# The last dense coefficient block kept in SBUF, and the expert stage's buffers moved, in a two-layer decoder trunk

## The chip, the cores and the metric

The kernel runs on one core of one Trainium2 chip. Its time is the device time of one launch in microseconds (us). Three runs of it are shown, and one further execution was recorded by the hardware profiler.

## What is computed

The reference is a decoder trunk of two layers on 512 tokens of width 1024, in f32. A layer is a mixer (sliding-window attention beside a convolution) and then PEER, a retrieval of single-neuron experts. The change touches only PEER and the code around it:

```python
def peer(h, w_query, sub_keys, u_tab, v_tab):
    q = (xt @ w_query).reshape(T, 8, 2, 128)
    s = einsum('thpd,hpnd->thpn', q, sub_keys)          # 128 keys per half
    ... top 16 of each half, top 16 of the pair sums -> ids (T, 8, 16), gates = softmax(top_s)
    a = gelu(einsum('chkd,cd->chk', u_tab[idc], xc))     # 16384 experts in all
    coef = gc * a
    return einsum('chk,chkd->cd', coef, v_tab[idc])
```

So each token uses 128 of 16384 experts (8 heads x 16), and expert (i, j) is row 128*i + j of the two tables.

## The kernel before, in words

**Two ways for PEER.** The first 128 tokens are done sparsely: GpSimd gathers the rows of their experts (`gather`, L484), VectorE takes the dot products (`dot`, L1290) and later the weighted sum (`weigh`, L1443). The other 384 tokens (`ND`) are done densely: all 128 tiles of the first table are multiplied with all dense tokens, and the coefficients of the experts that a token did not choose are zero.

**The U stage** has 128 tiles, U0 to U127. For each, SyncE loads 512 KB into one of four slots (`load`, L361, waits for the product four tiles earlier), ScalarE casts it to the high part `w_hi` (L756), VectorE or GpSimd makes the low part `w_lo` (L1406, L439), TensorE multiplies (24 matmuls of 384 columns, L526 to L528), ScalarE applies Gelu (L942) and stores the result to DRAM, `gelu_scratch` (L944). U0 to U31 run in a loop while VectorE works out the routes of the tokens. Then TensorE transposes the routes (L692), once for each of the three blocks of 128 dense tokens, and VectorE copies them out as `ijg` (L1416).

**The dense coefficients C** are built during U32 to U127, one block of 128 tokens in each 32 tiles. A block has 16 groups of 8 tokens. For a group VectorE writes one-hot matrices (L1428, L1429, L1431), TensorE multiplies them (L706), and ScalarE copies the result into `stage` (L967), 64 KB in each partition, `[i, j, token]`. TensorE and ScalarE do group g after tile `group_tile(g)`, whose offsets in a block are `k*27//16`: 0, 1, 3, 5, 6, 8, 10, 11, 13, 15, 16, 18, 20, 21, 23, 25. VectorE's order is written out by hand: before the one-hot matrices of a group it makes every `w_lo` up to the tile after the group's, and after them two or three of the dot products.

```python
while lows <= min(group_tile(g) + 1, NKEYS - 1):   # L1421
    u_low(lows); lows += 1
```

Two tiles after the last group of a block, SyncE starts to store `stage` to `c_scratch`, 2 MB behind each of four successive loads (L390). ScalarE may not write the first group of the next block until all four have landed (L963). TensorE runs these 96 tiles as a loop of three passes (`pe.Fori(0, NBD)`, L695), a pass being one block; SyncE loops likewise (L383).

**The V stage** (`experts`, L712) has 128 tiles too. For tile j SyncE fetches column j of C, 192 KB from `c_scratch`, and 192 KB of `gelu_scratch` into `cg` (`load_cg`, L392). VectorE multiplies the two into `coef` (`mix`, L1451), ScalarE casts `coef` to `cf_hi` (`coef_high`, L977), VectorE makes `cf_lo` (`mixed_low`, L1458) and the tile's `w_lo` (`weight_low`, L1464), and TensorE does 24 matmuls of 384 columns (L716 to L718) that add up in all eight PSUM banks. `cg`, `coef`, `cf_hi`, `cf_lo` and `y_sp` (the sparse sum) lie where `stage` was, at `base`, so the four stores of the last block have to land first: ScalarE waits for them at L972 and then sets `cg_free` by 4 (L973), which lets SyncE ask for the first columns. VectorE waits for a column, clears `y_sp` (L1480) and begins. During the first 96 V tiles the adaLN rows of the next norm are loaded too (`load_rows`, L366) and reduced by VectorE (`modulate`, L1029).

Of the kernel before, what the change touches and what calls it, by code (L numbers as in the profile page):

```python
# [44 lines left out]
C_TILES = 32  # L45
# [40 lines left out]
def group_tile(g):  # L86

    return U_ROUTE + C_TILES * (g // (P // GROUP)) + group_offset(g % (P // GROUP))


def group_offset(k):
    return k * 27 // 16
# [35 lines left out]
def build_trunk(nc, stream, u_rows, ada, params_d, keys_d, con_d, x_d, c_d, pos_d, c_scr, g_scr, out_d):  # L128
    with ExitStack() as ctx:
# [19 lines left out]
        xT = keep("xT", [P, C, T])  # L149
        h_hi = keep("h_hi", [P, C, T], F32R)  # L150
# [17 lines left out]
        sinT = keep("sinT", [P, T])  # L168
        rstd = keep("rstd", [P, T])
# [64 lines left out]
        cg = at("cg", base, [P, 4, 2, ND])  # L234
        coef = at("coef", base + 16 * KB, [P, 2, ND])
        cf_hi = at("cf_hi", base + 20 * KB, [P, 4, ND], F32R)
        cf_lo = at("cf_lo", base + 36 * KB, [P, 4, ND], F32R)
        y_sp = at("y_sp", base + 32 * KB, [P, D])
# [109 lines left out]
        def _(sp):  # L348
# [11 lines left out]
            with sp.Fori(0, DEPTH) as l:  # L360
# [5 lines left out]
                def load_rows(s, g, used):  # L366
                    n = sp.snap(g)
                    sp.wait_ge(mod_step, used)
                    sp.dma_start(rows[s][:], ada[n]).then_inc(ada_in[s], 16)
# [13 lines left out]
                with sp.Fori(0, NBD) as tb:  # L383
                    for k in range(C_TILES):
                        load(k % 4, l * NT + I_U + U_ROUTE + 4 + C_TILES * tb + k)
                        part = k - group_offset(P // GROUP - 1) - 2
                        if 0 <= part < 4:
                            to = sp.snap(tb + 0)
                            sp.wait_ge(c_ev, l * 2 * GROUPS + 2 * (P // GROUP) * tb + 2 * (P // GROUP) + 4)
                            sp.dma_start(c_scr[bass.ds(to, 1), :, 32 * part:32 * part + 32].rearrange("b i j t -> i (b j) t"),  # L390
                                         stage[:, 32 * part:32 * part + 32]).then_inc(c_st, 16)
                def load_cg(s, j, k):  # L392
                    jj = sp.snap(j)
                    sp.wait_ge(cg_free, k)
                    sp.dma_start(cg[:, s, 0].rearrange("i (b t) -> i b t", b=NBD),
                                 c_scr[:, :, bass.ds(jj, 1)].rearrange("b i o t -> i (b o) t")).then_inc(cg_in[s], 16)
                    sp.dma_start(cg[:, s, 1], g_scr[jj]).then_inc(cg_in[s], 16)


                for s in range(4):  # L400
                    load_cg(s, s, l * (NKEYS + 4) + s + 1)
                for n in range(ADA_2, ADA_2 + 3):
                    load_rows(n % 4, l * ADA_ALL + n, l * ADA_ALL + n - 2)

                def w_loads(r, rows_left=4):
                    for k in range(16):
                        load_cg(k % 4, 16 * r + k + 4, l * (NKEYS + 4) + 16 * r + k + 5)
                        if k % 4 == 0 and k // 4 < rows_left:
                            n = ADA_2 + k // 4 + 3
                            load_rows(n % 4, l * ADA_ALL + n + 4 * r, l * ADA_ALL + n - 2 + 4 * r)  # L410
                        load(k % 4, l * NT + I_W + 16 * r + k + 4)

                with sp.Fori(0, 3 * C // 4 - 1) as r:
                    w_loads(r)
                w_loads(3 * C // 4 - 1, 1)
# [91 lines left out]
        def _(pe):  # L507
            pe.wait_ge(const_in, 64)
            with pe.Fori(0, DEPTH) as l:
# [177 lines left out]

                u_tiles(0, U_ROUTE)
                for tt in range(1, NB):
                    pe.wait_ge(rt_ready, l * NBD + tt)  # L690
                    for k in range(3):
                        mm = nc.tensor.transpose(ps[:, 2 + tt, k * P:(k + 1) * P], routed[:, tt, k], ident)  # L692
                    mm.then_inc(rt_tr, 1)

                with pe.Fori(0, NBD) as tb:  # L695
                    g = 0
                    for k in range(C_TILES):
                        product(k % 4, l * NT + I_U + U_ROUTE + C_TILES * tb + k,
                                l * (NE // 2) + (I_U + U_ROUTE) // 2 + C_TILES // 2 * tb + k // 2 + 1, h_hi, h_lo, t0=P)
                        if g < P // GROUP and group_offset(g) == k:  # L700
                            pe.wait_ge(lr_done, l * GROUPS + P // GROUP * tb + g + 1)
                            for q in range(2):
                                pe.wait_ge(c_ev, l * 2 * GROUPS + 2 * (P // GROUP) * tb + 2 * g + q + 1)
                                for t in range(4):
                                    slot = GROUP * (g % 2) + 4 * q + t
                                    mm = nc.tensor.matmul(ps[:, 2 + (2 * g + q) % 4, t * P:(t + 1) * P],  # L706
                                                          oneL[:, slot], oneR[:, slot], start=True, stop=True)
                                mm.then_inc(c_mm, 1)
                            g += 1

# [869 lines left out]
```

## Time and profile before

| | |
|---|---|
| three runs, us | 4071.08, 4075.35 (median), 4086.86 |
| the profiled execution, us | 4082.31 |
| its span on the core, us | 4080.5 |
| granted TensorE clock, mean | 0.947 |
| TensorE matmul busy | 3671.6 us, 90% |
| TensorE weight load busy | 3286.8 us, 81% |
| VectorE busy | 3169.2 us, 78% |
| ScalarE busy | 1543.8 us, 38% |
| GpSimd busy | 1867.9 us, 46% |
| DMA | 895.76 MB, 220 GB/s mean |

The profile is of one execution, on the one core, and the other tables are taken from its trace. Engines are PE (TensorE matmul), PEld (its weight load), DVE (VectorE), ACT (ScalarE), POOL (GpSimd) and SP (SyncE); a name with q is that engine's instruction queue, where DMA issues show. A wait is put down to the instruction that ended it; "issue" stands where the profile shows nothing that the engine waited for. Starts are us from the start of the span. A matmul's recorded duration is longer than its share of the time, since matmuls overlap: their starts tell the pace. The same holds for VectorE instructions in a row, which start 0.08 us before the one ahead is shown to end.

### The profile page before, as it was taken

Reading aid. Unit: us, or ns where it says so; the run is one execution under the profiler, and the core shown is the slowest. Engines: PE = TensorE matmul, PEld = TensorE weight load, DVE = VectorE, ACT = ScalarE, POOL = GpSimd, SP = SyncE. Lnnn points to the kernel's source line nnn. Section 1 sums busy time; section 2 is a strip of 40 time slices with the busy share of each in tenths; the row PEclk is TensorE's granted clock in tenths of the full one; section 3 lists DMA queues with packets and bytes.
Section 4 is the critical chain, followed back from the end, with each engine's and each line's share of the span. In section 5 each row is a group of like instructions: output and inputs, shape, how many; then the busy total and the mean of one; then the engine's idle time right before and its main releaser. Section 6 shows DMA issues by size and latency. Waiting matters only on the chain.

```text
span 4080.5 us, 61011 instructions
## 1 busy us (share of the span) xinstructions
PE 3671.6 (90%) x19042; PEld 3286.8 (81%) x19042; DVE 3169.2 (78%) x5223; ACT 1543.8 (38%) x2201; POOL 1867.9 (46%) x1324
## 2 busy tenths in 40 slices
PE   4888888998999969999978888889989999699998
PEld 2655666898999969999955556668989999699998
DVE  6888952799877958888768889328997979588887
ACT  3344233344444433333343332433444544233332
POOL 3211455365544645555432115544744646455553
PEclk9887999999999989999998779999999999899999
DMA  5410122256898899999933102223669898999997
GB/s 197 145 37 31 67 68 87 81 182 195 272 319 312 280 346 377 370 377 357 339 120 114 37 27 76 69 86 98 183 208 313 288 325 285 359 377 374 373 351 280
DMA packets 368728, 895.76 MB, mean 220 GB/s; under 512 B 33665, under 2 KB 197505, under 8 KB 364929
## 3 DMA queue, kind: packets, MB, share of 16 engines
q1 hardware_dynamic: 257632, 572.25, 40.8%
q0 software_dynamic: 73728, 268.47, 19.0%
q10 hardware_dynamic: 37152, 52.45, 3.5%
q8 instruction: 102, 1.67, 0.2%
q14 instruction: 114, 0.93, 0.1%
HBM read 790.27 MB, written 102.76 MB: 219 GB/s over the span
## 4 chain that ended last, share of the span: by engine, by line
PE 39%; issue 31%; DVE 14%; POOL 9%; DMA 6%; ACT 1%; SPq 0%; POOLq 0%; DVEq 0%; ACTq 0%
PE ps L716 8%; PE ps L718 8%; PE ps L717 8%; POOL w_lo L439 7%; PE ps L528 4%; PE ps L527 4%; PE ps L526 4%; DMA raw<-stream 3%; PE ps L706 3%; DVE i L1308 2%; DVE eq L1375 1%; DMA c_scratch<-stage 1%; DVE eq L1368 1%; DVE v L1304 1%; DMA cg<-gelu_scratch 1%
## 5 line engine op out<-in xcount | busy, mean ns | idle before, releaser
L526 PE MATMUL ps<-h_hi,w_hi 128*128 128x384 f32 (+1 forms) x3008 | 1115.2, 371 | 96.1 <-POOL h_lo L446 41.9
L439 POOL TENSOR_TENSOR w_lo<-raw,w_hi 128x1024 fp32r<-128x1024 f32 x232 | 638.3, 2760 | 1010.6 <-ACT w_hi L756 998.8
L527 PE MATMUL ps<-h_lo,w_hi 128*128 128x384 f32 (+1 forms) x3008 | 1078.4, 358 | 0.0
L528 PE MATMUL ps<-h_hi,w_lo 128*128 128x384 f32 (+1 forms) x3008 | 1076.8, 358 | 0.0
L756 ACT CAST w_hi<-raw 128x1024 fp32r<-128x1024 f32 x680 | 714.0, 1054 | 930.1 <-DMA raw<-stream 883.2
L716 PE MATMUL ps<-cf_hi,w_hi 128*128 128x384 f32 x2048 | 688.4, 336 | 67.8 <-DVE cf_lo L1461 65.9
L502 POOL TENSOR_TENSOR spare<-spare 128x1 f32<-128x1 f32 x504 | 282.9, 561 | 962.4 <-DVE y_sp L1448 487.4
L526 PEld LDWEIGHTS ps<-h_hi,w_hi 128*128 128x128 f32 x3008 | 578.9, 192 | 178.4 <-issue 52.1
L718 PE MATMUL ps<-cf_hi,w_lo 128*128 128x384 f32 x2048 | 685.9, 335 | 0.0
L717 PE MATMUL ps<-cf_lo,w_hi 128*128 128x384 f32 x2048 | 685.9, 335 | 0.0
L527 PEld LDWEIGHTS ps<-h_lo,w_hi 128*128 128x128 f32 x3008 | 580.1, 193 | 43.8 <-issue 8.0
L528 PEld LDWEIGHTS ps<-h_hi,w_lo 128*128 128x128 f32 x3008 | 577.7, 192 | 42.2
L487 POOL DMA_INDIRECT gbuf<-stream,ids_v x256 | 444.2, 1735 | 39.2 <-issue 2.6
L716 PEld LDWEIGHTS ps<-cf_hi,w_hi 128*128 128x128 f32 x2048 | 385.9, 188 | 73.9 <-DVE w_lo L1467 73.4
L487 POOL DMA_INDIRECT gbuf<-u_rows,ids_u x256 | 407.8, 1593 | 39.8 <-POOL spare L502 5.0
L717 PEld LDWEIGHTS ps<-cf_lo,w_hi 128*128 128x128 f32 x2048 | 385.9, 188 | 0.0
L718 PEld LDWEIGHTS ps<-cf_hi,w_lo 128*128 128x128 f32 x2048 | 385.7, 188 | 0.0
L1406 DVE TENSOR_TENSOR w_lo<-raw,w_hi 128x1024 fp32r<-128x1024 f32 x192 | 233.3, 1223 | 168.6 <-ACT w_hi L756 168.5
L1296 DVE CUSTOM_DVE_ANT_1 gbuf<-gbuf,h_tok 128x1024 f32<-128x1024 f32 x256 | 302.2, 1220 | 43.7 <-DMA gbuf<-u_rows,ids_u 43.7
L1448 DVE SCALAR_TENSOR_TENSOR y_sp<-gbuf,a_sp,y_sp 128x1024 f32<-128x1024 f32 x256 | 327.3, 1279 | 0.0
L1467 DVE TENSOR_TENSOR w_lo<-raw,w_hi 128x1024 fp32r<-128x1024 f32 x256 | 311.8, 1218 | 0.0
L942 ACT ACTIVATE g_out<-ps 128x384 f32<-128x384 f32 x256 | 125.8, 492 | 486.1 <-PE ps L528 474.8
(209 smaller groups left out, 4720.5 us busy)
## 6 DMA issues: line engine op xcount, KB each, us to landing
raw<-stream SPq DMA_DIRECT2D x680, 512.0 KB, 5.2
rows<-ada SPq DMA_DIRECT2D x112, 512.0 KB, 5.8
gelu_scratch<-g_out ACTq DMA_DIRECT2D x256, 192.0 KB
c_scratch<-stage SPq DMA_DIRECT2D x24, 2048.0 KB, 16.7
cg<-c_scratch SPq DMA_DIRECT2D x256, 192.0 KB, 5.4
cg<-gelu_scratch SPq DMA_DIRECT2D x256, 192.0 KB, 5.9
gbuf<-u_rows,ids_u POOLq DMA_INDIRECT x256, 6.6
gbuf<-stream,ids_v POOLq DMA_INDIRECT x256, 7.4
```

The costliest lines, as they stand in the source:

```text
L439: nc.gpsimd.tensor_tensor(w_lo[:, s], raw[:, s], w_hi[:, s].bitcast(F32), ALU.subtract).then_inc(lo_done, 1)
L487: nc.gpsimd.indirect_dma_start(out=gbuf[:, n % SLOTS], out_offset=None, in_=table, in_offset=bass.IndirectOffsetOnAxis(ap=ids[:, k:k + 1], ...
L526: nc.tensor.matmul(ps[:, b, 0:n], wh, hi[:, c, t0:T], start=c == 0, stop=False)
L527: nc.tensor.matmul(ps[:, b, 0:n], wh, lo[:, c, t0:T], start=False, stop=False)
L528: mm = nc.tensor.matmul(ps[:, b, 0:n], wl, hi[:, c, t0:T], start=False, stop=c == C - 1)
L716: nc.tensor.matmul(ps[:, c, P:T], w_hi[:, s, c], cf_hi[:, s], start=first, stop=False)
L717: nc.tensor.matmul(ps[:, c, P:T], w_hi[:, s, c], cf_lo[:, s], start=False, stop=False)
L718: mm = nc.tensor.matmul(ps[:, c, P:T], w_lo[:, s, c], cf_hi[:, s], start=False, stop=last)
L756: nc.scalar.copy(w_hi[:, s], raw[:, s]).then_inc(hi_done, 1)
L1296: nc.vector.tensor_tensor_reduce(out=row, in0=row, in1=h_tok[:, :, 0:P], scale=1.0, scalar=0.0, op0=ALU.mult, op1=ALU.add, accum_out=a_sp[ ...
L1448: nc.vector.scalar_tensor_tensor(out=y_sp[:], in0=gbuf[:, k % 4], scalar=a_sp[:, bass.ds(at_k, 1)], in1=y_sp[:], op0=ALU.mult, op1=ALU.add ...
L1467: nc.vector.tensor_tensor(w_lo[:, k % 4], raw[:, k % 4], w_hi[:, k % 4].bitcast(F32), ALU.subtract).then_inc(lo_done, 1)
```

## The change

1. The last of the three blocks of C is no longer stored. `c_scratch` has two blocks (`STORED`), the third stays in `stage`, and `mix` does two multiplications: 256 tokens from `cg`, 128 from the column of `stage`.
2. The V stage's buffers leave the place of `stage`: `cg` and `coef` to where the one-hot matrices were, `cf_hi` and `cf_lo` beside them and into `rstd` and `h_lo`, `y_sp` into `h_lo`, and the adaLN rows of the V stage (`w_rows`) into `h_hi`. The rows can be asked for only after the last U product, so `load_rows` goes behind `load` in the V stage, and `modulate` from the first to the last tile of four.
3. ScalarE sets `cg_free` after the last group, and SyncE asks for the first four columns during the last four U tiles. The waits of TensorE for banks 0 and 1 go to the last chunks of the first V tile. `coef_high(0, 0)` comes ahead of the Gelu of `a_sp` and ahead of the wait for the last stores of `gelu_scratch`; VectorE clears `y_sp` and finishes `a_sp` behind the first `mixed_low`.
4. The routes are transposed after U34 in place of after U31.
5. The groups of the blocks begin at tiles 36, 66 and 96 (before 32, 64 and 96), at offsets `k*23//16`: 0, 1, 2, 4, 5, 7, 8, 10, 11, 12, 14, 15, 17, 18, 20, 21.
6. The loops of TensorE and SyncE over the blocks are written out: no jump back at U64 and U96.

```diff
 def group_tile(g):
-    return U_ROUTE + C_TILES * (g // (P // GROUP)) + group_offset(g % (P // GROUP))
+    return C_FIRST[g // (P // GROUP)] + g % (P // GROUP) * 23 // 16
...
-        cg = at("cg", base, [P, 4, 2, ND])
-        coef = at("coef", base + 16 * KB, [P, 2, ND])
...
-        y_sp = at("y_sp", base + 32 * KB, [P, D])
+        cg = at("cg", base + 74 * KB, [P, 4, NS + ND])
+        coef = at("coef", base + 84 * KB, [P, 2, ND])
...
+        y_sp = at("y_sp", h_lo_base, [P, D])
+        w_rows = [at(f"w_rows{k}", h_hi_base + 4 * KB * k, [P, D]) for k in range(4)]
...
-                    sp.dma_start(cg[:, s, 0].rearrange("i (b t) -> i b t", b=NBD),
+                    sp.dma_start(cg[:, s, 0:NS].rearrange("i (b t) -> i b t", b=STORED),
                                  c_scr[:, :, bass.ds(jj, 1)].rearrange("b i o t -> i (b o) t")).then_inc(cg_in[s], 16)
...
-                for s in range(4):
-                    load_cg(s, s, l * (NKEYS + 4) + s + 1)
...
+                for u in range(U_ROUTE + 4, NKEYS + 4):
+                    load(u % 4, l * NT + I_U + u)
+                    for tb in range(STORED):
+                        part = u - 4 - group_tile((tb + 1) * (P // GROUP) - 1) - 2
+                        if 0 <= part < 4:
+                            sp.wait_ge(c_ev, l * 2 * GROUPS + 2 * (P // GROUP) * (tb + 1) + 4)
+                            sp.dma_start(c_scr[tb, :, 32 * part:32 * part + 32],
+                                         stage[:, 32 * part:32 * part + 32]).then_inc(c_st, 16)
+                    if u >= NKEYS:
+                        load_cg(u - NKEYS, u - NKEYS, l * (NKEYS + 4) + u - NKEYS + 1)
...
+                for u in range(U_ROUTE, NKEYS):
+                    u_tile(u)
+                    if u == U_ROUTE + 2:
+                        for tt in range(1, NB):
+                            pe.wait_ge(rt_ready, l * NBD + tt)
...
+                    while g < GROUPS and group_tile(g) == u:
+                        c_group(g)
+                        g += 1
+                W_ORDER = tuple(range(2, C)) + (0, 1)
...
+                    for c in W_ORDER:
+                        if first and c < 2:
+                            pe.wait_ge(bank_read[c], (l + 1) * (NE // 2) + 1)
...
-                act.wait_ge(c_st, (l + 1) * (NBD * 64) + 64)
-                nc.scalar.copy(st4[:, 4], st4[:, 3]).then_inc(cg_free, 4)
...
+                        if g == GROUPS:
+                            nc.scalar.copy(st4[:, 4], st4[:, 3]).then_inc(cg_free, 4)
...
+                coef_high(0, 0)
                 act.wait_ge(row_used, l * 2 * P + P + 4)
                 nc.scalar.activation(a_sp[:], a_sp[:], ACT.Gelu).then_inc(a_gelu, 1)
...
                 u_low(U_ROUTE + 1)
-                lows = U_ROUTE + 2
+                u_low(U_ROUTE + 2)
+                lows = U_ROUTE + 3
...
-                    nc.vector.tensor_tensor(coef[:, k % 2], cg[:, k % 4, 0], cg[:, k % 4, 1],
-                                            ALU.mult).then_inc(cg_free, 1)
+                    nc.vector.tensor_tensor(coef[:, k % 2, 0:NS], cg[:, k % 4, 0:NS], cg[:, k % 4, NS:2 * NS], ALU.mult)
+                    nc.vector.tensor_tensor(coef[:, k % 2, NS:], stage[:, bass.ds(j, 1)].rearrange("i o t -> i (o t)"),
+                                            cg[:, k % 4, 2 * NS:], ALU.mult).then_inc(cg_free, 1)
```

## Rows read from the trace of the kernel before

**Rows 1.** All waits of PE, whole span: us in total, times, longest
```profile
PE ps L716 <- DVE cf_lo L1461: 65.9, 2, 33.5
...
PE ps L706 <- DVE oneR L1431: 18.2, 22, 1.8
...
PE ps L526 <- issue: 11.8, 3, 4.7
```
**Rows 2.** The chain that ended last, in order of time: start us, us, what
```profile
987.39 1.78 PE ps L706 x16
...
1151.05 3.10 PE ps L706 x16
...
1476.84 28.67 DMA c_scratch<-stage
```
**Rows 3.** Waits from 1477 to 1514, then the same from 3491 to 3529
```profile
ACT st L973 <- DMA c_scratch<-stage: 13.8, 1, 13.8
...
PE ps L716 <- DVE cf_lo L1461: 32.4, 1, 32.4
```
**Rows 4.** Timelines of SP, DVE and PE around the first V tile
```profile
1505.81 0.40 SPq L395 DMA_DIRECT2D cg<-c_scratch  x1
...
1513.05 0.55 DVE L1461 TENSOR_TENSOR cf_lo<-coef,cf_hi 128x384 fp32r<-128x384 f32 x1
...
1513.73 0.68 PE L716 MATMUL ps<-cf_hi,w_hi 128*128 128x384 f32 x1 [33.49 <-DVE cf_lo L1461]
```
**Rows 5.** Timeline of ACT, U58 to U67: Gelus, casts and copies
```profile
1112.62 0.49 ACT L942 ACTIVATE g_out<-ps 128x384 f32<-128x384 f32 x1 [2.19 <-PE ps L528]
1113.14 0.34 ACTq L944 DMA_DIRECT2D gelu_scratch<-g_out  x1
1113.52 1.05 ACT L756 CAST w_hi<-raw 128x1024 fp32r<-128x1024 f32 x1 [0.41 <-ACT g_out L942]
1116.78 0.49 ACT L942 ACTIVATE g_out<-ps 128x384 f32<-128x384 f32 x1 [2.21 <-PE ps L528]
...
1137.12 1.05 ACT L756 CAST w_hi<-raw 128x1024 fp32r<-128x1024 f32 x1 [5.83 <-DMA raw<-stream]
...
1145.20 1.05 ACT L756 CAST w_hi<-raw 128x1024 fp32r<-128x1024 f32 x1 [6.64 <-DMA raw<-stream]
...
1152.96 1.05 ACT L756 CAST w_hi<-raw 128x1024 fp32r<-128x1024 f32 x1 [0.53 <-DMA raw<-stream]
```
**Rows 6.** DMA issues with sizes: KB, median us from issue to landing
```profile
cg<-gelu_scratch SPq DMA_DIRECT2D x256, 192.0 KB, 5.9
```
**Rows 7.** Timeline of DVE, one group of the first block
```profile
1020.28 1.22 DVE L1428 TENSOR_TENSOR oneR<-con,ijg 128x1024 f32<-128x1024 f32 x1
1021.41 1.22 DVE L1429 TENSOR_TENSOR oneL<-con,ijg 128x1024 f32<-128x1024 f32 x1
```
**Rows 8.** Timeline of SP: the loads and stores behind U61 and U62
```profile
1129.40 0.33 SPq L364 DMA_DIRECT2D raw<-stream  x1
1130.22 0.80 SPq L390 DMA_DIRECT2D c_scratch<-stage  x1
1133.56 9.87 SPq L364 DMA_DIRECT2D raw<-stream  x2
```
**Rows 9.** Timeline of PE from 1136 to 1152: the start of U64
```profile
1136.89 0.44 PE L526 MATMUL ps<-h_hi,w_hi 128*128 128x384 f32 x1 [3.51 <-issue]
```
**Rows 10.** Timeline of PE and DVE around the transposes of the routes
```profile
952.36 0.82 PE L692 MATMUL ps<-con,routed 128*128 128x128 f32 x6
962.82 0.90 PE L692 MATMUL ps<-con,routed 128*128 128x128 f32 x3 [9.64 <-DVE routed L1396]
963.95 0.69 PE L526 MATMUL ps<-h_hi,w_hi 128*128 128x384 f32 x1 [0.23 <-DVE w_lo L1406]
...
964.95 1.48 DVE L1416 COPY ijg<-ps 128x384 f32<-128x384 f32 x3
```
**Rows 11.** Busy time by stretch, 1514 to 2051: PE, PEld, DVE, ACT, POOL, clock, DMA, GB/s
```profile
1514.00:2051.00 537.00, 535.82 (x3074) 533.58 (x3075) 450.34 (x563) 186.88 (x254) 277.43 (x250) 1.00 1.00 359
```

More of the change, by code:

```diff
@@ L44 @@
 U_ROUTE = 32
-C_TILES = 32
+C_FIRST = (36, 66, 96)
+STORED = NBD - 1
+NS = STORED * P
 EXP_TILES = (6, 14, 22, 29)
@@ L381, in _ @@
                         load(s, l * NT + 4 * r + s)
[L383 to L391, printed above, removed]
                 def load_cg(s, j, k):
@@ L406, in w_loads @@
+                def w_loads(r, first=False, rows_left=4):
                     for k in range(16):
                         load_cg(k % 4, 16 * r + k + 4, l * (NKEYS + 4) + 16 * r + k + 5)
+                        load(k % 4, l * NT + I_W + 16 * r + k + 4)
+                        for n in range(3) if first and k == 0 else ():
+                            load_rows(n, l * ADA_ALL + ADA_2 + n, l * ADA_ALL + ADA_2 + n - 2, w_rows)
                         if k % 4 == 0 and k // 4 < rows_left:
                             n = ADA_2 + k // 4 + 3
-                            load_rows(n % 4, l * ADA_ALL + n + 4 * r, l * ADA_ALL + n - 2 + 4 * r)
@@ L686, in u_tiles @@
                                     l * (NE // 2) + (I_U + u0) // 2 + 2 * r + s // 2 + 1, h_hi, h_lo, t0=P)
-                u_tiles(0, U_ROUTE)
[L689 to L709, printed above, removed]
@@ new lines, in u_tile, with c_group @@
+                def u_tile(u):
+                    product(u % 4, l * NT + I_U + u, l * (NE // 2) + (I_U + u) // 2 + 1, h_hi, h_lo, t0=P)
+                def c_group(g):
+                    pe.wait_ge(lr_done, l * GROUPS + g + 1)
+                    for q in range(2):
+                        pe.wait_ge(c_ev, l * 2 * GROUPS + 2 * g + q + 1)
+                        for t in range(4):
+                            slot = GROUP * (g % 2) + 4 * q + t
+                            mm = nc.tensor.matmul(ps[:, 2 + (2 * g + q) % 4, t * P:(t + 1) * P],
+                                                  oneL[:, slot], oneR[:, slot], start=True, stop=True)
+                        mm.then_inc(c_mm, 1)
@@ L714, in experts @@
                     pe.wait_ge(lo_done, g + 5)
-                    for c in range(C):
-                        nc.tensor.matmul(ps[:, c, P:T], w_hi[:, s, c], cf_hi[:, s], start=first, stop=False)
-                        nc.tensor.matmul(ps[:, c, P:T], w_hi[:, s, c], cf_lo[:, s], start=False, stop=False)
-                        mm = nc.tensor.matmul(ps[:, c, P:T], w_lo[:, s, c], cf_hi[:, s], start=False, stop=last)
+                    for c in W_ORDER:
+                        if first and c < 2:
+                            pe.wait_ge(bank_read[c], (l + 1) * (NE // 2) + 1)
+                        nc.tensor.matmul(ps[:, c, P:T], w_hi[:, s, c], cf_hi[s][:], start=first, stop=False)
+                        nc.tensor.matmul(ps[:, c, P:T], w_hi[:, s, c], cf_lo[s][:], start=False, stop=False)
+                        mm = nc.tensor.matmul(ps[:, c, P:T], w_lo[:, s, c], cf_hi[s][:], start=False, stop=last)
                     mm.then_inc(tile_done, 1)
-                for b in range(2):
-                    pe.wait_ge(bank_read[b], (l + 1) * (NE // 2) + 1)
+                pe.wait_ge(h_ev, 2 * l + 2)
                 pe.wait_ge(c_ev, (l + 1) * 2 * GROUPS + 4)
```

84 lines of the change are left out of this document (43 added, 41 removed).

## The prediction

> **What bounds the kernel now.** I read the waits of TensorE over the whole span first. The longest that lie near the change are 65.9 us in 2 times in front of the first V matmul, 18.2 us in 22 times of group matmuls for one-hot matrices, and 11.8 us in 3 times put down to issue [rows 1]. The reader is to see that the V stage itself is not at fault: from 1514 to 2051 TensorE is busy 535.82 of 537.00 us at a clock of 1.00, although the DMA share is 1.00 as well [rows 11]. So a gain has to come from the seam between the stages, and a loss can come from the U stage, where VectorE and the loads run close behind TensorE.
>
> The chain of waits says what the seam is made of: the last quarter of `stage` goes to DRAM for 28.67 us [rows 2], ScalarE waits for it 13.8 us, and only then is the first column asked for, at 1505.81 [rows 3, 4]. V0 starts at 1513.73 after 33.49 us of nothing [rows 4], and 32.4 us in layer 2 [rows 3].
>
> **Part 1, the seam.** The last stores go away, and with them what queued behind them. New order: the first column is asked for when U124 is done, three tiles or 3 x 4.16 = 12.5 us before U127 ends (tile pace: 1116.78 - 1112.62 [rows 5]); a column half lands in 5.9 us [rows 6], so it is there in time. Call T0 the end of U127. ScalarE must do the Gelu of U127 before `coef_high(0, 0)`: its start is some 0.2 us behind T0, and the next ScalarE instruction starts 0.90 us later [rows 5]. I take the cast to `cf_hi` at `cf_lo`'s 0.55 us; then `cf_lo` itself, 0.55, and 0.13 to the matmul [rows 4]. Sum 0.2 + 0.9 + 0.55 + 0.55 + 0.15 = 2.35, say 2.4 us. V1 has a second small wait that I expect: ScalarE now stands at the wait for the last stores of `gelu_scratch` with `coef_high(1)` queued behind it, and VectorE's `cf_lo(1)`, `w_lo(1)` behind that. No row has that store's landing; the nearest is the 5.9 us of a load of the same size [rows 6]. Store issued at T0 + 0.7, landed T0 + 6.6, cast 0.55, `cf_lo` 0.55, `w_lo` 1.2, small gaps: V1 at T0 + 9.1, where V0 ends at 2.4 + 4.2 = 6.6. That is 2.5 us; bounds 0 (lands in 3 us) and 5 (lands late among saturated DMAs). New idle time 4.9 us a layer. Gain 33.5 - 4.9 = 28.6 and 32.4 - 4.9 = 27.5: **-56.1 us**, bounds -47 and -61. The first V matmul after the long wait is recorded 0.68 us long [rows 4], the first of U64 after 3.51 us idle 0.44 us [rows 9]; whether two short waits cost a slow start as well I can't tell, so I book 0 for it, bounds -4 and 0.
>
> **Part 2, closer groups.** VectorE instructions of this size follow each other by 1.14 us (1020.28 to 1021.41) [rows 7]. A group costs 3 one-hots and 118/48 = 2.46 dot products, 6.2 us, plus 1.14 for each `w_lo`. Where the next group is one tile on, VectorE needs 7.4 us and TensorE 4.16 + 1.78 = 5.9 [rows 2]: it falls 1.4 us behind. Two tiles on it needs 8.5 against 10.1 and makes up 1.6. Before, a block has 5 close and 10 wide steps, a surplus. After, 9 close and 6 wide: 9 x 1.4 - 6 x 1.6 = 3 us short over each block, and twice a block (0, 1, 2 and 10, 11, 12) two close steps come in a row. The wait is on record: 18.2 us over 30 close steps, 0.61 us each [rows 1]. 54 close steps at 0.61 give 32.8: **+14.6 us**. Lower bound: only the throughput counts, 6 blocks x 3 = 18, so 0. Upper bound: no lead is ever made, 54 x 1.4 = 76, so +58. I take 0.61 because the wide steps before and after still refill the lead.
>
> **Part 3, the stores of blocks 1 and 2 meet other tiles.** The stores still fall behind the four loads after the last group. U65, U66 and U67 arrive late in the same queue: their casts start at 1137.12, 1145.20 and 1152.96 [rows 5], about 7.9 us apart, against 4.16 for a tile; the last load left at 1133.56 behind a store [rows 8]. Before, groups 16 and 17 (tiles 64 and 65) use up two pieces of that dead time, 3.6 us of real work; group 17 starts at 1151.05 and takes 3.10 [rows 2]. After, nothing is there to do until tile 66, and group 16's one-hots stand behind `w_lo(67)` in VectorE's order. U63 ended at about 1133.4 (1136.89 - 3.51 [rows 9]). With the same arrivals: U65 can start at 1139.4 and U66 at 1147.5 (cast + 1.05 + 1.2); `w_lo(67)` is done at 1155.2, the one-hots 3.4 later, group 16 at 1158.7 to 1160.5, U67 ends 1164.7. Before, U66 and U67 follow group 17, 1154.15 + 2 x 4.16 and some 0.4 of slow start = 1162.9, with one group more done, worth 1.8. Loss 1.8 + 1.8 = 3.6 us. The same geometry holds at tile 96 (stores four tiles ahead of the first group in both), and in both layers: 4 x 3.6 = **+14.4 us**. Bounds: 0, if the arrivals come earlier because no gathers run then, and +20, with slow-clock starts after the longer wait. ScalarE's own wait for the stores ahead of the first group goes away; it hides under the loads, so nothing.
>
> **Part 4, routes later.** U32 does not start earlier: it waits for `w_lo(32)` on VectorE (963.95, 0.23 us after the last transposes) [rows 10]. The 9 transposes, 0.82 for 6 [rows 10], now lie bare after U34: 1.2 us; VectorE idles until then, copies `ijg` (0.5 until the last), and only then makes `w_lo(35)`, 1.2, with hand-overs 2.0 us of wait. Removed: two short waits of groups 0 and 1, 0.8. Net 2.4 x 2 = **+4.8 us**, bounds 0 and 8.
>
> **Part 5, with one answer.** SyncE's written-out order adds no DMA; 256 columns fetch 64 KB less and 4 x 2 MB x 2 of stores are gone: DMA has no wait of TensorE's in V, so 0, bounds -3 and 0. The split multiplication adds one instruction a tile, at most the 0.55 of the whole width [rows 4]; VectorE is idle (537 - 450)/128 = 0.68 us a tile [rows 11], so 0. If that cover were gone, each 0.1 us of it would cost 256 x 0.1 = 26 us. The three or four row loads that once ran in the dead time now come after V0, 2 MB at 359 GB/s [rows 11] or some 6 us, against four slots of 4.16 us: 0, bounds 0 and 6. Clearing `y_sp` and finishing `a_sp` lie under V0.
>
> **Part 6, loops written out.** TensorE idles 3.51 us in front of U64 with nothing it waited for on record, just where its loop jumps back [rows 9], 11.8 us in 3 times over both layers [rows 1]. By the Trainium skill (Runtime: NRT & Kernel Launch, Instruction fetch mechanics) a taken branch to a page that is not held forces a fetch before execution goes on, while straight code is fetched ahead. The trace agrees as to the place; by that rule alone the sum would be 11.8 us lower. I book 0, since by part 3 U65's and U66's weights would then be what is late.
>
> **The sum.** -56.1 + 14.6 + 14.4 + 4.8 = -22.3 us. The profiled execution has 4082.31 us, 1.8 around its span of 4080.5; it would come to 4060. It lies 7 us above the median of the runs, so from the median: 4075.35 - 22.3 = 4053 us.
>
> **Rivals.** 0.5% is 20.4 us, about what a measurement of this kernel can tell from no change. (a) *The U stage gives nothing back.* The seam is worth 56, the stores' stalls don't grow, and the jumps' 11.8 us come home as well: the idle time before U64 is then the jump's own, not a cover over late loads. For it: 3.51 us after data that was ready. Against: casts 7.9 us apart. Time: 4075 - 56 - 12 + 15 + 5 = 4027. (b) *The wait only moves.* The first V tiles start without the head start that 33 us gave the four slots, and run at the landing times of loads and columns under a DMA share of 1.00; some 10 us a layer go there. Time 4053 + 20 = 4073. For it: DMA share 1.00 [rows 11]; against: TensorE almost never waits there. (c) *VectorE becomes the bound of the dense blocks, slower than before.* Place: one-hot matrices behind `w_lo` in a fixed order. Price: each close step waits its full 1.4 us, +58 in place of +14.6. Time 4053 + 43 = 4096. It decides against the change from a mean wait per close step of about 1.03 us ((18.2 + 22.3 + 14.6)/54). Against: 0.61 now. (d) *The change doesn't do what it says*: if the columns or `cg_free` stayed behind another wait (the dot products' end, say), the seam would stay above 20 us and the sum near 0; the code shows no such wait. It goes with (b).
>
> **How the numbers follow.** Forecast as summed, 4053 (4035 to 4068): 0.48. (a) 4027: 0.25. (b) and (d) 4073: 0.2. (c) 0.07. Faster by over 0.5% (below 4055): just over half of the forecast and all of (a) and a little of (b), 0.55. Within 0.5%: 0.37. Slower: 0.08. Range: 4020 to 4077 leaves out the tails of (a) and (c).
>
> **What would show it.** Wait of L716's successor before V0: 2 to 3 us, a second of 0 to 5 before V1. Waits of the group matmuls for `oneR`: 25 to 40 us over the span in place of 18.2. In front of U65 to U67 and group 16, some 12 us idle in place of 9. A wait of about 2 us before U35. No "issue" waits in front of U64 and U96. Wrong would be: a seam above 10 us, one-hot waits above 60 us, or U stages as long as before.

## The result, and the profile after

Over twenty runs of each, the changed kernel has a median of 4097.38 us (4082.66 to 4115.73) and the kernel before 4085.11 us (4067.69 to 4096.37). The ratio is 1.0031, 95% interval 1.0019 to 1.0043: slower by 0.3%, a difference that the interval keeps apart from zero but that is under the 0.5% that the prediction took as no change. The forecast was 4053 us and its range ended at 4077, so the measured time lies outside. The profiled execution has 4094.12 us and a span of 4091.9, 11.4 us more than the span of before.

The page of after, span, busy times and DMA:

```profile
span 4091.9 us, 61289 instructions
...
PE 3681.5 (90%) x19042; PEld 3289.0 (80%) x19042; DVE 3188.8 (78%) x5479; ACT 1544.3 (38%) x2203; POOL 1935.0 (47%) x1324
...
DMA packets 334805, 862.13 MB, mean 211 GB/s; under 512 B 33536, under 2 KB 164608, under 8 KB 332032
```

895.76 MB have become 862.13, so 34 MB less are moved, and yet nothing is gained. All waits of PE in after, whole span (us in total, times, longest), those that answer to [rows 1]:

```profile
PE ps L528 <- DVE w_lo L1414: 44.7, 12, 11.5
PE ps L701 <- DVE oneR L1440: 42.1, 32, 8.4
...
PE ps L727 <- DVE w_lo L1475: 27.8, 24, 5.4
```

The 65.9 us in front of V0 are gone from the top. In their place stand a wait inside the V stage for the low part of the weights (27.8 in 24 times), twice the wait for one-hot matrices (42.1 for 18.2), and waits of the U stage for `w_lo`. No wait of the dense U tiles is put down to issue any more. Of the 42.1, 24.2 stand in front of groups 16 and 32, the first ones of the second and third block, over both layers; the 17.9 in front of all other groups are no more than the 18.2 of before. (Of the 44.7, 11.5 a layer stand in front of U32 and answer to the 9.64 in front of the routes in [rows 10].)

To see where the time went, I cut each layer at three starts in the timeline of PE: the first matmul of U32, of V0, and the first transpose of `y_sp`, which ends the V stage. "Wait" is the idle time just ahead of V0.

| us, layer 1 / layer 2 | before | after | after - before |
|---|---|---|---|
| U32 to the end of U127 | 516.3 / 511.5 | 532.2 / 533.0 | +15.9 / +21.5 |
| wait ahead of V0 | 33.5 / 32.4 | 2.4 / 2.3 | -31.1 / -30.1 |
| V stage | 537.1 / 538.8 | 558.8 / 552.3 | +21.7 / +13.5 |

The sum is +11.4 us, and that is the difference of the spans; what lies ahead of U32 cancels (it is 6.5 us longer in layer 1 and 6.6 shorter between the layers). The seam gave 61.2, a little more than was forecast. The U stage gave 37.4 back, forecast 33.8. The V stage, at which the forecast put nothing of its own, took 35.2. Only 1.0 of it in each layer is the short wait of V1, which the forecast counted with the seam. By the timeline of PE, waits inside the two V stages grew from 1.8 to 27.8 us, that is 26.0 of the 35.2; the other 9 lie in matmuls without a wait that start more than the usual 0.173 us apart, behind such waits or at the lower clock. Timeline of PE in after, the waits at the start of the V stage of layer 1 (start us, us, what, idle before):

```profile
1505.10 0.44 PE L727 MATMUL ps<-cf_hi,w_hi 128*128 128x384 f32 x1 [2.43 <-DVE cf_lo L1469]
...
1512.17 0.44 PE L727 MATMUL ps<-cf_hi,w_hi 128*128 128x384 f32 x1 [1.04 <-DVE w_lo L1475]
...
1530.33 0.69 PE L727 MATMUL ps<-cf_hi,w_hi 128*128 128x384 f32 x1 [5.40 <-DVE w_lo L1475]
```

What VectorE waits for there is in its own timeline and in that of SP's queue:

```profile
1511.30 0.34 SPq L367 DMA_DIRECT2D raw<-stream  x1
1511.84 1.92 SPq L372 DMA_DIRECT2D w_rows<-ada  x4
1513.88 0.39 SPq L389 DMA_DIRECT2D cg<-c_scratch  x1
...
1526.65 0.43 DVE L1462 TENSOR_TENSOR coef<-cg 128x256 f32<-128x256 f32 x1 [7.86 <-DMA cg<-gelu_scratch]
```

Four adaLN rows (2 MB) go out together, and the next column is asked for behind them. `mix` then waits 7.86 us for a column; in VectorE's order the `mix` of tile k+2 stands ahead of the `mixed_low` and `weight_low` of tile k+1, so TensorE waits 5.40 us. It isn't only the start. Busy time by stretch (PE, PEld, DVE, ACT, POOL, clock, DMA share, GB/s) in the middle of the stage, first before, then after:

```profile
1600.00:1700.00 100.00, 99.09 (x571) 98.77 (x571) 84.53 (x107) 35.22 (x48) 52.09 (x48) 1.00 1.03 374
1700.00:1800.00 100.00, 100.00 (x576) 99.48 (x576) 86.67 (x110) 34.95 (x48) 53.20 (x49) 1.00 1.03 375
1800.00:1900.00 100.00, 100.00 (x576) 99.50 (x575) 86.88 (x110) 35.31 (x49) 52.45 (x49) 1.00 1.02 368
```

```profile
1600.00:1700.00 100.00, 97.21 (x554) 95.61 (x554) 83.18 (x127) 33.77 (x46) 58.23 (x46) 1.00 0.98 345
1700.00:1800.00 100.00, 95.47 (x542) 93.33 (x541) 84.25 (x129) 34.21 (x46) 50.01 (x45) 1.00 0.96 344
1800.00:1900.00 100.00, 96.75 (x554) 95.48 (x553) 85.43 (x129) 33.59 (x45) 53.42 (x48) 1.00 0.96 341
```

Before, TensorE starts 1723 matmuls in these 300 us, after only 1650. At the pace of the full stretches (100 us for 576) the 73 that are missing are worth 12.7 us. The clock is 1.00 in all of them, so in these stretches it is not that.

### The profile page after: what moved, and what is told of

Same layout as the page of the kernel before. It is cut to its first block, busy times and chain, and to the rows that moved or that the text cites. A ratio compares the mean times of both kernels' runs of the same rounds, so it can differ in the third digit from the quotient of the medians.

```text
span 4091.9 us, 61289 instructions
## 1 busy us (share of the span) xinstructions
PE 3681.5 (90%) x19042; PEld 3289.0 (80%) x19042; DVE 3188.8 (78%) x5479; ACT 1544.3 (38%) x2203; POOL 1935.0 (47%) x1324
## 2 busy tenths in 40 slices
DMA packets 334805, 862.13 MB, mean 211 GB/s; under 512 B 33536, under 2 KB 164608, under 8 KB 332032
## 4 chain that ended last, share of the span: by engine, by line
issue 35%; PE 30%; DVE 14%; POOL 13%; DMA 6%; SPq 1%; ACT 1%; DVEq 0%; POOLq 0%; ACTq 0%
POOL w_lo L441 10%; PE ps L727 7%; PE ps L729 6%; PE ps L728 6%; DMA cg<-gelu_scratch 4%; PE ps L528 3%; PE ps L530 3%; PE ps L529 3%; PE ps L701 2%; DMA raw<-stream 2%; DVE gbuf L1304 2%; DVE i L1316 2%; DVE oneR L1437 2%; DVE oneR L1440 2%; DVE v L1312 1%
## 5 line engine op out<-in xcount | busy, mean ns | idle before, releaser
L528 PE MATMUL ps<-h_hi,w_hi 128*128 128x384 f32 (+1 forms) x3008 | 1113.6, 370 | 123.7 <-DVE w_lo L1414 44.7
L504 POOL TENSOR_TENSOR spare<-spare 128x1 f32<-128x1 f32 x504 | 325.6, 646 | 905.4 <-DVE y_sp L1454 460.9
L727 PE MATMUL ps<-cf_hi,w_hi 128*128 128x384 f32 x2048 | 691.7, 338 | 33.1 <-DVE w_lo L1475 27.8
L489 POOL DMA_INDIRECT gbuf<-u_rows,ids_u x256 | 430.4, 1681 | 39.7 <-issue 3.5
```

Source lines behind the costliest of these rows:

```text
L489: nc.gpsimd.indirect_dma_start(out=gbuf[:, n % SLOTS], out_offset=None, in_=table, in_offset=bass.IndirectOffsetOnAxis(ap=ids[:, k:k + 1], ...
L504: nc.gpsimd.tensor_tensor(spare[:, 16:17], spare[:, 17:18], spare[:, 18:19], ALU.add).then_inc(room, 1)
L528: nc.tensor.matmul(ps[:, b, 0:n], wh, hi[:, c, t0:T], start=c == 0, stop=False)
L727: nc.tensor.matmul(ps[:, c, P:T], w_hi[:, s, c], cf_hi[s][:], start=first, stop=False)
```

## The experiments

Two theories for the V stage. **Q**, the place in SyncE's queue: before, the rows stand behind the next column and ahead of the next weight load; in the changed kernel they stand behind the weight load and so ahead of the next column. **H**, the head start (rival (b) of the prediction): the 33 us of dead time let the first loads and columns land, and without it the stage runs from hand to mouth. A third, **M**, blames the new layout or the split multiplication. For the U stage the suspects are those of parts 2 to 4. Eleven kernels ran, with 4 to 12 executions each. rows_spread, closer_alone, both_spread and third_closer ran on another chip than the rest; each ratio is to the kernel before on the same chip, whose median was 4083.04 us there and 4081.95 and 4083.07 here.

**rows_behind**: the changed kernel with the order of before in the V stage.

```diff
-                        load(k % 4, l * NT + I_W + 16 * r + k + 4)
-                        for n in range(3) if first and k == 0 else ():
+                        for n in range(3) if first and k == 1 else ():
...
-                        if k % 4 == 0 and k // 4 < rows_left:
+                        if k % 4 == 1 and k // 4 < rows_left:
...
+                        load(k % 4, l * NT + I_W + 16 * r + k + 4)
```

> The changed kernel, but in the V stage each 512 KB of adaLN rows is asked for behind the next column and ahead of the next weight tile (as before the change), one tile later than in the changed kernel. Theory Q (queue order: since the change the rows stand ahead of the next column in SyncE's queue, the column lands late and VectorE waits for it ahead of a weight's low part): the V stage of layer 1 falls from 558.9 us to 537 to 545, waits of TensorE in it from 17 to under 7 us, the whole time by 20 to 35 us. Theory H (head start: the V stage suffers because its first tiles no longer begin with four landed columns and weights): the V stage stays at 553 to 560. Theory M (the split multiplication, more VectorE work in each tile): the same as H.

Measured: 4078.94 us, ratio to before 0.9977 (0.9961 to 0.9993). V stage 549.6 and 542.2 us against 558.8 and 552.3: 9 and 10 us come back in the layers, and TensorE's waits for the low weights fall from 27.8 to 16.1 us. So the order is a cause, but not all of theory Q came: the V stage of layer 1 is still 12 us longer than before, outside the 537 to 545 that were expected, and the time fell by 18.4 us where 20 to 35 were.

**groups_as_before**: the changed kernel with the groups at tiles 32, 64 and 96, offsets `k*27//16`, and the routes transposed after U31; the loops stay written out.

```diff
-C_FIRST = (36, 66, 96)
+C_FIRST = (32, 64, 96)
...
-    return C_FIRST[g // (P // GROUP)] + g % (P // GROUP) * 23 // 16
+    return C_FIRST[g // (P // GROUP)] + g % (P // GROUP) * 27 // 16
```

> The changed kernel with the groups at tiles 32, 64 and 96 with offsets k*27//16 and the routes transposed after U31, as before the change; loops still written out. By my parts 2 to 4 the tiles U32 to U127 take 516 us in layer 1 again (532.2 in the changed kernel), 512 in layer 2 (533.0), one-hot waits fall from 42.1 to about 18 us over the span, the whole by 30 to 38 us. Rival: the stretch does not depend on where the groups lie (only on the written-out loop or on DMA), and stays above 526 us. The V stage stays as long as in the changed kernel.

Measured: 4074.39 us, 0.9984 (0.9967 to 1.0001). U32 to the end of U127 takes 515.0 and 512.8 us, as before the change; so the new order of the groups and routes holds all that the U stage lost. But V0 now waits 9.8 and 8.9 us, since the last groups come after tile 121 and VectorE still has dot products to do. The V stage stays at 560.1 and 558.3. One expectation failed: the one-hot waits come to 34.3 us and not to about 18. 17.7 of them stand in front of groups 16 and 32, right behind U64 and U96, ahead of which the kernel before has its waits put down to issue; the rest, 16.6, is about the 18.2 of before.

**both_back**: the two edits together.

> Both of the above together. If the two effects are independent and each as large as expected, the whole is 55 to 65 us below the changed kernel, so about 40 to 55 us (1.0 to 1.3%) below the kernel before: the seam alone, some 60 us for both layers, is then what the idea is worth. If the head start matters (theory H), it is only 15 to 25 us below the kernel before.

Measured: 4055.14 us, 0.9933 (0.9910 to 0.9957), faster than both kernels. V stage 547.5 and 545.5. The two effects add (18.4 and 23.0 us alone, 42.2 together, against the changed kernel). Against the kernel before, 26.8 us are gained, less than the 40 to 55 expected and just above the 15 to 25 of theory H. Its timelines of SP and DVE behind V0:

```profile
1494.20 2.13 SPq L372 DMA_DIRECT2D w_rows<-ada  x4
...
1510.41 0.43 DVE L1460 TENSOR_TENSOR coef<-cg 128x256 f32<-128x256 f32 x1 [7.22 <-DMA cg<-gelu_scratch]
```

The column behind the burst of four rows is late here too, whichever the burst's place in the queue; that it is the burst and not theory H, rows_spread shows.

**loop_written_out**: the kernel before with TensorE's loop over the blocks written out (`pe.Fori(0, NBD)` becomes `range(NBD)`), nothing else.

> The kernel before with nothing changed but TensorE's loop over the three blocks written out. If the 11.8 us of waits put down to issue in front of U64 are the jump's own, they go and the whole falls by up to 12 us. If they only cover late loads (my part 3), the issue waits are replaced by waits for low parts or one-hot matrices of about the same size, and the whole stays within 4 us.

Measured: 4083.14 us, 1.0009 (0.9991 to 1.0027): no difference. The waits put down to issue (11.8 us) are gone, and those for one-hot matrices rise from 18.2 to 35.6, of which 20.2 stand in front of groups 16 and 32, right behind the places of the jump. The jump back only covered late loads, as part 6 had it.

**rows_spread**: rows_behind, and one row in each four tiles from the first on, in place of four at once.

```diff
-                        for n in range(3) if first and k == 1 else ():
-                            load_rows(n, ...)
-                        if k % 4 == 1 and k // 4 < rows_left:
-                            n = ADA_2 + k // 4 + 3
+                        if k % 4 == 1:
+                            n = ADA_2 + k // 4
```

> The changed kernel, with the adaLN rows of the V stage asked for behind the next column and ahead of the next weight load (as in rows_behind), and besides that one row in each four tiles from the first on, in place of four rows (2 MB) at once behind V tile 1. Theory B (the burst starves the first V tiles): the 5 us wait of TensorE in the first ten V tiles is gone, no wait there is over 2.5 us, and the V stage comes to 540 to 545 us in layer 1 and 537 to 541 in layer 2, against 549.6 and 543.0 of rows_behind; time some 8 to 14 us under rows_behind, near 4067. Theory H (missing head start: only four columns and weights are on hand at V0, whatever the rows do): the wait stays at 3 us or more and moves a few tiles, the V stage stays at 547 to 551 and 542 to 545; time near 4077.

Measured: 4073.98 us, 0.9963 (0.9947 to 0.9979). The V stage is 540.2 and 539.4 us, no wait for the low weights inside it is over 1.4 us, and they come to 6.2 us in all. By the V stage theory B holds: what head start was missing costs no more than the scatter once the rows are out of the way. By the time it holds less well: it falls by some 5 us against rows_behind, where 8 to 14 were expected and the V stages explain 12. U32 to V0 takes 542.3 and 538.2 us in this execution, 4 and 1 longer; in layer 1 V0 waits 6.63 us, as `mix` waits for its column.

**before_rows_ahead**: the counterpart on the kernel before, with all its head start: one swap.

```diff
+                        load(k % 4, l * NT + I_W + 16 * r + k + 4)
                         if k % 4 == 0 and k // 4 < rows_left:
                             n = ADA_2 + k // 4 + 3
                             load_rows(n % 4, l * ADA_ALL + n + 4 * r, l * ADA_ALL + n - 2 + 4 * r)
-                        load(k % 4, l * NT + I_W + 16 * r + k + 4)
```

> The kernel before, with one swap: in the V stage the adaLN rows are asked for behind the weight load and so ahead of the next column, as the changed kernel does; the three rows ahead of V0, the buffers and all else as before. V stage of before: 537.1 and 538.8 us. Theory Q (the place in the queue costs 9 to 10 us a layer by itself, as undoing it gave in rows_behind and both_back): 546 to 549, ratio to before 1.004 to 1.005. Theory H (it costs only where the stage begins short, with columns asked for late and four rows at once): 537 to 541, ratio 0.999 to 1.001.

Measured: 4103.88 us, 1.0053 (1.0037 to 1.0070). V stage 553.7 and 550.9 against 537.1 and 538.8, that is +16.6 and +12.1, most of the +21.7 and +13.5 of the whole change and more than the 9 to 10 expected. (The profiled execution lies 7 us above its median; by the medians the swap costs 20.8 us.) The seam is untouched (33.9 and 32.3). This parts the theories: the order alone does most of it, with the old buffers, the single multiplication and the full head start, so neither M nor H is needed for that part. All waits of PE, and the same 100 us as above:

```profile
PE ps L716 <- DVE w_lo L1467: 20.3, 20, 2.3
...
1700.00:1800.00 100.00, 96.92 (x544) 93.45 (x543) 80.62 (x103) 33.34 (x46) 50.04 (x46) 1.00 1.02 356
```

The DMA share is 1.02 here and 1.03 before, yet 32 matmuls fewer start. The share says that the queue is full in both; it does not say whose turn it is. The queue of SP shows that, first before, then with the swap:

```profile
1700.93 0.38 SPq L395 DMA_DIRECT2D cg<-c_scratch  x1
1701.49 0.34 SPq L397 DMA_DIRECT2D cg<-gelu_scratch  x1
1702.10 0.53 SPq L369 DMA_DIRECT2D rows<-ada  x1
1704.50 0.33 SPq L364 DMA_DIRECT2D raw<-stream  x1
```

```profile
1694.99 0.33 SPq L364 DMA_DIRECT2D raw<-stream  x1
1695.58 0.33 SPq L369 DMA_DIRECT2D rows<-ada  x1
1696.18 0.38 SPq L395 DMA_DIRECT2D cg<-c_scratch  x1
1696.75 0.34 SPq L397 DMA_DIRECT2D cg<-gelu_scratch  x1
...
1703.79 0.56 DVE L1455 TENSOR_TENSOR coef<-cg 128x384 f32<-128x384 f32 x1 [2.35 <-DMA cg<-gelu_scratch]
```

SyncE waits for a tile to end before each weight load. Before, the row is issued in that pause, with the column already asked for and 2.4 us ahead of the weights. With the swap, weights, row and column go out within 1.8 us, and the column, wanted first, comes last.

**closer_alone**: groups at 32, 64 and 96 and routes as before, but the closer offsets.

> The changed kernel, with the groups at tiles 32, 64 and 96 and the routes transposed after U31 as before, but the closer offsets k*23//16 kept. It parts the closer groups from the later beginning. From the start of U32 to that of V0 it was 534.7 and 535.3 us in the changed kernel and 524.8 and 521.7 in groups_as_before, whose V0 waits 9.8 and 8.9 us. Theory S (the prediction's price, 0.61 us for each close step, 7.3 us a layer): 523 to 526 in both layers, with V0 waiting under 3 us, and the later beginning with its stores and routes holds the other 10 to 12 us. Theory C (the closeness alone costs it all, VectorE too late in every block): 531 to 536. Times: S 4072 to 4080, C near 4095. The V stage is that of the changed kernel, 553 to 560.

Measured: 4064.16 us, 0.9952 (0.9936 to 0.9969), below the 4072 to 4080 of theory S. U32 to V0 takes 525.7 and 527.9 us, V0 waits 2.3: theory S by its size, 2 us over its upper end in layer 2. Without the wait of V0, against groups_as_before, that is +8.4 and +12.8 for the closeness, and the wait of V0 gets back 7.5 and 6.6 of it. But the price is not made as the prediction had it. All waits of PE, first groups_as_before, then closer_alone:

```profile
PE ps L701 <- DVE oneR L1438: 34.3, 28, 4.6
...
PE ps L528 <- DVE w_lo L1413: 0.6, 3, 0.2
```

```profile
PE ps L528 <- DVE w_lo L1413: 25.5, 14, 3.3
...
PE ps L701 <- DVE oneR L1438: 22.4, 37, 2.3
```

The one-hot waits don't grow, they fall. What grows are the waits of U tiles for their low parts, and nearly all of them stand in front of U61 to U63 and U93 to U95: the closer blocks end four tiles earlier, so the loads that are late behind the stores are now those of tiles with no groups beside them.

**routes_early**: the changed kernel with the routes transposed after U31.

> The changed kernel, with the routes transposed after U31 as before and nothing else. From U32 to V0 it was 534.7 and 535.3 us in the changed kernel, and 525.7 and 527.9 in closer_alone, which differs from this one in the later beginning of the first two blocks alone. Theory R (prediction: routes later cost 2.4 us a layer, the later beginning with its stores the rest): 531 to 534 in both layers, and the waits behind the stores (1.4, 3.0, 4.8 us at U65, U66 and group 16) stay. Rival (the routes hold it all, by putting VectorE behind for the whole of the first block): 525 to 528, and those waits shrink below 1 us each. The V stage is that of the changed kernel, 552 to 559. Times: R near 4092, rival near 4080.

Measured: 4092.93 us, 1.0034 (1.0005 to 1.0062). U32 to V0 is 535.8 and 532.2, so theory R: the routes cost -1 and +3 us, within the scatter, and the later beginning of the first two blocks the other 9.8 and 4.3 (against closer_alone, without the wait of V0). Timeline of PE in routes_early and then in closer_alone, group 16:

```profile
1138.18 0.44 PE L528 MATMUL ps<-h_hi,w_hi 128*128 128x384 f32 x1 [2.11 <-DVE w_lo L1413]
1145.00 0.45 PE L528 MATMUL ps<-h_hi,w_hi 128*128 128x384 f32 x1 [0.78 <-DVE w_lo L1413]
1155.12 3.77 PE L701 MATMUL ps<-oneR,oneL 128*128 128x128 f32 x16 [5.69 <-DVE oneR L1438]
```

```profile
1165.66 2.05 PE L701 MATMUL ps<-oneR,oneL 128*128 128x128 f32 x16 [0.25 <-DVE oneR L1438]
```

With the first block ended at tile 53, the loads behind the stores are those of U59 to U62 and done with by group 16; their price was paid at U61 to U63. With its end at 57 they are U63 to U66, and the low part of U67 stands ahead of group 16's one-hot matrices in VectorE's order.

**both_spread**: groups and routes as before, rows spread.

> Groups and routes as before, and the adaLN rows spread as in rows_spread. Theory B: against both_back (4055.1; V stage 547.5 and 546.3; one wait of 5 us 28 us behind V0 in each layer) the wait goes, V stage 541 to 544; time 4044 to 4050. Theory H: no change from both_back, within 3 us.

Measured: 4039.22 us, 0.9903 (0.9877 to 0.9928). V stage 536.6 and 543.0; V0 waits 11.4 and 8.2.

**third_closer**: both_spread with the closer offsets in the third block alone.

> As both_spread, but with the closer offsets k*23//16 in the third block alone, so that its last group comes after tile 117 in place of 121. V0 waits 11.0 and 11.6 us in both_back, since VectorE still has dot products to do. If the end of the groups sets when VectorE is through with them, V0 waits 2 to 4 us and the third block loses a third of the 7.3 us a layer priced for three blocks: from U32 to V0 516 to 520 us against 524.1 and 523.4, time 10 to 14 us under both_spread. If the gathers of the dot products set it (VectorE waits for them three times in the last 10 us), V0 still waits 8 us or more and the time is within 5 us of both_spread.

Measured: 4038.88 us, 0.9892 (0.9865 to 0.9919). V0 waits 2.3 us in both layers and U32 to V0 takes 519.5 and 519.0, as expected, but the time is that of both_spread: the V stages are 545.3 and 538.4, and the waits for one-hot matrices 38.7 us against 33.3. The expected 10 to 14 us did not come. The stages explain a gain of 6 and a loss of 4; that the loss belongs to the edit is not shown, since it has the opposite sign in the two layers.

**dots_earlier**: both_spread with 122 in place of 118 dot products between the groups.

```diff
-DOTS_BY_GROUP = 118
+DOTS_BY_GROUP = 122
```

> As both_spread (groups and routes as before, rows spread), with 122 in place of 118 dot products put between the groups of U32 to U127, so that 6 and not 10 are left behind the last group. V0 waits 11.4 and 8.2 us in both_spread. If VectorE's leftover dot products set that wait: V0 waits 3 to 7 us, and the four dot products spread over 48 groups (4 x 1.22 us a layer) cost up to 2 us in the waits for one-hot matrices: from U32 to V0 517 to 521 against 522.8 and 522.0; time 4030 to 4037. If the gathers set it: unchanged within 1.5 us, as gathers come at their own pace.

Measured: 4028.08 us, 0.9866 (0.9833 to 0.9900), the lowest median of all. V0 waits 2.3 and 4.1, U32 to V0 is 520.1 and 518.8, V stage 541.7 and 542.8. The leftover dot products set V0's wait; that much is shown. A gain in the whole time against both_spread is not: the stages up to V0 explain 6 us, the V stages take back 5, the profiled execution (4042.4 us of span) is no shorter than that of both_spread (4038.8), there are four executions of each, on different chips, and the intervals of the two ratios overlap.

**The V stages side by side.** Several of the thirteen kernels share the code of the V stage, so it was measured more than once (us, both layers):

| adaLN rows asked for | kernels | lowest to highest | mean |
|---|---|---|---|
| as in the kernel before | before, loop_written_out | 537.1 to 542.3 | 540.1 |
| the same, swapped | before_rows_ahead | 550.9 to 553.7 | 552.3 |
| as in the changed kernel | after, groups_as_before, closer_alone, routes_early | 552.3 to 561.0 | 556.5 |
| behind the column, four at once | rows_behind, both_back | 542.2 to 549.6 | 546.2 |
| behind the column, spread | rows_spread, both_spread, third_closer, dots_earlier | 536.6 to 545.3 | 540.9 |

Equal code differs by up to 9 us, so one pair of executions can't carry a few us. The means can be compared: of the 16.4 us that a layer lost, the place in the queue holds 10.3, the burst 5.3, and 0.8 is left for the head start, the layout and the split multiplication together, well within the scatter.

## Why the prediction was wrong

- **Part 1, the seam: right.** The wait before V0 is 2.43 us (forecast 2.4), before V1 1.04 (forecast 2.5, bounds 0 to 5). With V1's wait counted the gain is about 59 us against 56.1. The slow start that was booked at 0 is there, but it was there before too: V0 takes 6.0 us in both layers of after, without V1's wait, and took 5.8 and 7.0 before, where a tile at full clock takes 4.16. The short waits bring it as the long ones did.
- **Part 2, closer groups: the size is near, the mechanism was another.** Forecast +14.6, shown 8.4 and 12.8, so 21.2. It was priced as one-hot waits, 0.61 us for each close step, and those hardly grew: closer_alone has 22.4 us, and the changed kernel 17.9 beside groups 16 and 32, against 18.2 before, though the close steps went from 30 to 54. What grew is part 3's mechanism, waits for low parts behind the stores (25.5 us in closer_alone, 0.6 in groups_as_before), as the blocks end four tiles earlier. That the size is near is luck. The test named for it, one-hot waits of 25 to 40 us, gave 42.1, but tests something else: without closer groups they are 34.3, as the written-out loop no longer covers the waits of groups 16 and 32. What the prediction did not see is that this price also buys part of part 1: without the closer groups V0 waits 9 to 11 us for the dot products.
- **Part 3, the stores: right.** Forecast +14.4, shown 9.8 and 4.3, so 14.1. The waits in after are 1.42, 2.97 and 4.84 us in front of U65, U66 and group 16, 9.2 in sum where some 12 were expected.
- **Part 4, routes later: no more than scatter.** Forecast +4.8, shown +2.1 in sum, with opposite signs in the layers. The wait in front of U35 is there with 2.25 us (forecast 2.0).
- **Part 5 is the step that failed.** It said of the row loads "0, bounds 0 and 6", weighing their 2 MB against four slots, and it booked "DMA has no wait of TensorE's in V". The order in which SyncE asks for the rows was changed in the same edit, and that was priced nowhere. It cost 16.6 and 12.1 us by itself on the kernel before (20.8 by the medians), and with the burst at the start the V stages of after are 21.7 and 13.5 longer. Forecast 0, measured 35.2: that is the whole miss: -22.3 + 35.2 = +12.9, where the medians differ by 12.3, and what the other parts missed (-5.1 at the seam, +3.6 in the U stage) nearly cancels. The multiplication in two pieces was rightly put at 0: in rows_spread it is there, and the V stage is that of before within 3 us.
- **Part 6, loops written out: right.** The waits put down to issue went, in loop_written_out and in after alike, and in loop_written_out nothing was gained. By the rule of the Trainium skill (Runtime: NRT & Kernel Launch, Instruction fetch mechanics) a taken branch out of the pages that are held forces a fetch first. The place of the wait agrees with it, but by that rule alone 11.8 us should have come home, and the interval around 1.0009 leaves room for less than 4.
- **The rivals.** (a) is excluded by the U stage's 37.4 us. (b) was right that TensorE's wait comes back in the V stage, and had over half of the size: 10 us a layer against 17.6. Its cause was not the right one: before_rows_ahead has the full head start and loses most of the same, rows_spread has none and loses next to nothing. (c) did not come: the mean over 54 close steps is 17.9/54 = 0.33 us, and 0.78 even with groups 16 and 32 counted, under the 1.03 from which it would decide. (d) is excluded, the seam is gone.

The evidence against the 0 of part 5 was at hand: a DMA share of 1.00 with TensorE waiting for nothing [rows 11] is a balance that rests on the order of the queue, and I read it as slack.

## What to carry to other kernels

Where the DMA share is 1.00 and the bound engine still does not wait, the order of the queue may be what keeps it so, as it was here: price every transfer that changes its place, even if no byte is added. Put a transfer that nobody wants soon behind what is wanted next and into a pause in which the issuing engine waits anyway, and spread such transfers, one for several tiles, in place of a burst. And when a seam closes, look for what closes it: here VectorE's leftover work is next in line, and moving four dot products ahead shortened the way to V0 as much as closer groups in the third block.

## What the runs showed of the hardware

- **A full DMA share hides the order.** With the swap alone the share of 1700 to 1800 goes from 1.03 to 1.02 and the moved rate from 375 to 356 GB/s, as fewer tiles are done in the time; the loss shows in TensorE's waits for low weights, 20.3 us against 1.8, and not in the share.
- **The clock after a wait.** In both_back TensorE idles for 11.02 us ahead of V0, and the granted clock of 1485 to 1491 is 0.50. The first V matmuls (timeline of PE) start 0.32 us apart, from 1491.10 on 0.17 to 0.19 apart: the lower and then the higher of the two levels (1.2 and 2.4 GHz). The first 18 take 5.92 us in place of 3.1, which is 2.8 us on top of the wait:

```profile
1485.18 0.68 PE L726 MATMUL ps<-cf_hi,w_hi 128*128 128x384 f32 x1 [11.02 <-DVE cf_lo L1467]
1485.66 0.52 PE L727 MATMUL ps<-cf_lo,w_hi 128*128 128x384 f32 x1
...
1490.78 0.49 PE L728 MATMUL ps<-cf_hi,w_lo 128*128 128x384 f32 x1
1491.10 0.35 PE L726 MATMUL ps<-cf_hi,w_hi 128*128 128x384 f32 x1
```

  After the 5.40 us at 1530.33 in the changed kernel the granted clock of 1530 to 1534 is 0.53. A short wait can do it too: behind the 2.43 us ahead of V0 in after, the first seven matmuls start at the full pace and then the clock falls (0.57 over 1506 to 1510):

```profile
1506.09 0.34 PE L729 MATMUL ps<-cf_hi,w_lo 128*128 128x384 f32 x1
1506.26 0.34 PE L727 MATMUL ps<-cf_hi,w_hi 128*128 128x384 f32 x1
...
1506.72 0.52 PE L729 MATMUL ps<-cf_hi,w_lo 128*128 128x384 f32 x1
1507.04 0.52 PE L727 MATMUL ps<-cf_hi,w_hi 128*128 128x384 f32 x1
...
1509.92 0.34 PE L727 MATMUL ps<-cf_hi,w_hi 128*128 128x384 f32 x1
```

  The length of the wait alone does not tell the price. Before, 33.5 and 32.4 us ahead of V0 were followed by 10 and 18 matmuls at the lower level; in layer 2 of rows_behind, waits of 2.31 and 2.99 us ahead of V0 and V1 were followed by none, with a granted clock of 1.00 over 3522 to 3530.
- **Equal work, unequal stages.** The same code of the V stage takes up to 9 us more or less from layer to layer and from one profiled execution to the next (552.3 to 561.0, 536.6 to 545.3), and the time of one kernel varies by 10 us and more between executions. Smaller differences in single stages are told here as they stand and not explained.
